# Sharing the gathered value rows between TensorE and VectorE while the second block's coefficients are spread

## The reference, cut to what matters

```
tv, tp = top_k(cand, 16)                    # 8 heads x 16 experts = 128 experts per token
gw = softmax(tv)
a  = einsum('td,ted->te', x, expert_u[ids]) # 128 dot products per token
a  = gelu(a) * gw                           # 128 coefficients per token
out = einsum('te,ted->td', a, expert_v[ids])
```

## Time and profile before

| | |
|---|---|
| median of 3 runs | 2955.72 us (2953.44 to 2956.95) |
| the profiled execution | span 2956.1 us, 0.4 us above the median |
| burst, first to last spreading of block 1 | 2424.8 to 2501.4 us |
| dense product alone on TensorE | 2502.1 to 2936.4 us |
| last instruction of DVE ends | 2953.1 us |

### The profile page before, as it was taken

One profiled execution on the slowest core, in us unless ns is written; L12 is line 12 of the kernel. 1 busy time (PEld: TensorE's weight loads), 2 busy tenths in 40 slices (PEclk: granted clock), 3 DMA queues, 4 the chain that ended last, 5 costly groups with the idle time before them and its releaser, 6 DMA issues.

```text
span 2956.1 us, 31045 instructions
## 1 busy us (share of the span) xinstructions
PE 2663.8 (90%) x11792; PEld 2070.4 (70%) x11792; DVE 2160.4 (73%) x2978; ACT 607.8 (21%) x1271; POOL 894.0 (30%) x712
## 2 busy tenths in 40 slices
PE   6999889999999999999999999667676758999997
PEld 5888678866587588478657688667666755666665
DVE  6787476577896747524677769999999878656667
ACT  1121240110110110122000021122377776000000
POOL 1100001000000100000000024777767657656664
PEclk8999999999999999999999999888877779999998
DMA  9954469868787834324978769999999988999998
GB/s 402 421 190 153 152 226 409 352 247 355 287 319 300 311 128 143 142 100 153 361 279 321 268 273 416 421 421 421 413 421 421 403 338 283 403 410 414 414 414 349
DMA packets 147736, 935.12 MB, mean 316 GB/s; under 512 B 16400, under 2 KB 16656, under 8 KB 53136
## 3 DMA queue, kind: packets, MB, share of 16 engines
q0 software_dynamic: 101376, 604.02, 51.1%
q1 hardware_dynamic: 44784, 320.66, 28.0%
q10 hardware_dynamic: 1440, 8.59, 0.7%
HBM read 929.02 MB, written 4.19 MB: 316 GB/s over the span
## 4 chain that ended last, share of the span: by engine, by line
PE 58%; DMA 19%; DVE 8%; ACT 7%; POOL 5%; issue 3%; DVEq 0%; SPq 0%; ACTq 0%
PE G L579 32%; PE M L894 7%; DMA acc<-v_rows,proj 6%; PE B L894 3%; DMA mix<-v_rows,proj 3%; DMA vec<-peer_u,proj 3%; ACT vec L1576 2%; DMA aring<-peer_u,proj 2%; PE M L1162 2%; DMA proj<-v_rows,proj 2%; DVE vec L2512 2%; PE G L894 2%; POOL aring L551 1%; PE G L1150 1%; POOL acc L563 1%
## 5 line engine op out<-in xcount | busy, mean ns | idle before, releaser
L579 PE MATMUL G<-h,ring 128*128 128x256 f32 x3264 | 715.6, 380 | 0.5 <-ACT h L1298 0.2
L579 PEld LDWEIGHTS G<-h,ring 128*128 128x128 f32 x3264 | 616.1, 190 | 91.6 <-issue 6.8
L536 POOL DMA_DIRECT2D aring<-ada x176 | 93.2, 530 | 1493.7 <-DVE mods L1707 1445.4
L1707 DVE CUSTOM_DVE_ANT_0 aring<-aring,acc,vec 128x2048 f32<-128x2048 f32 x160 | 372.2, 2350 | 49.9 <-DMA aring<-ada 46.8
L579 PE MATMUL G<-proj,ring 128*128 128x256 f32 x1472 | 322.1, 380 | 0.9 <-DVE proj L2324 0.9
L579 PEld LDWEIGHTS G<-proj,ring 128*128 128x128 f32 x1472 | 279.6, 191 | 41.4 <-issue 3.4
L1209 PE MATMUL M<-sq,mix 128*128 128x512 f32 x688 | 301.4, 594 | 0.0
L551 POOL DMA_INDIRECT aring<-peer_u,proj x130 | 228.6, 1759 | 197.2 <-DVE dots L2484 83.3
L1209 PEld LDWEIGHTS M<-sq,mix 128*128 128x128 f32 x688 | 203.6, 297 | 89.3 <-ACT mix L1590 0.7
L2512 DVE SCALAR_TENSOR_TENSOR vec<-acc,dots,vec 128x1024 f32<-128x1024 f32 x149 | 191.5, 1285 | 97.1 <-DMA acc<-v_rows,proj 91.8
L2484 DVE CUSTOM_DVE_ANT_0 aring<-sq,aring 128x2048 f32<-128x2048 f32 x104 | 236.4, 2290 | 29.1 <-DMA aring<-peer_u,proj 18.7
(11 more groups left out here) (494 smaller groups left out, 3670.5 us busy)
## 6 DMA issues: line engine op xcount, KB each, us to landing
ring<-weights SPq DMA_DIRECT2D x219, 1024.0 KB, 5.3
aring<-ada POOLq DMA_DIRECT2D x176, 1024.0 KB, 8.6
sq<-v_blocks SPq DMA_DIRECT2D x43, 1024.0 KB, 8.0
proj<-v_blocks SPq DMA_DIRECT2D x21, 1024.0 KB, 8.0
ring<-first SPq DMA_DIRECT2D x16, 896.0 KB, 11.2
sq<-ada POOLq DMA_DIRECT2D x8, 1024.0 KB, 20.9
acc<-ada POOLq DMA_DIRECT2D x4, 1024.0 KB, 19.4
proj<-ada POOLq DMA_DIRECT2D x4, 1024.0 KB, 22.9
```

The costliest lines, as they stand in the source:

```text
L536: pool.dma_start(ada_at(n), ada[n]).then_inc(ada_in[ada_slot(n)], 16)
L579: mm = nc.tensor.matmul(bank[:, 0:TOK], lhsT=ring[:, slot, weights_at + t * P:weights_at + (t + 1) * P], rhs=rhs[:, t, :], start=(t == ord ...
L1707: V_.tensor_tensor_reduce(out=tile, in0=tile, in1=vector, scale=1.0, scalar=bias, op0=ALU.mult, op1=ALU.add, accum_out=column).then_inc(ad ...
```

## The change

Of block 0's rows, TensorE adds 16 in the burst (the odd rows 1 to 31), one half row in every group. DVE adds the even rows 0 to 30, one in every second group. So the burst adds 32 rows, and the 8 rows from 32 to 39 are added behind it. DVE makes the diagonals instead of ACT, with four buffers instead of two: four of them during the dots (at rows 234 to 240), the others in the burst. DVE marks the one-hot matrices of groups 0 and 1 during the dots (at rows 243 and 247); for that the expert numbers of block 1 are turned ahead of row 239 instead of behind the last row. The diagonal of row 244 is read at row 255 instead of 252. ACT runs a one-column gelu at row 222, right behind the softmax's exponential.

```
+READ_BEHIND[TURN_LATE[-1]] = 255
-V_ON_PE = [4 + 5 * i for i in range(8)]
+V_ON_PE = [1 + 2 * i for i in range(16)]
+IN_BURST = 2 * len(V_ON_PE)
+PICKS_TURNED_AT = TURN_LATE[-2]
+MARKED_AT = {243: 0, 247: 1}
+DIAGS_AT = {234: 0, 236: 1, 238: 2, 240: 3}
+DIAGS = 4
...
 # TensorE: turn_picks(1) ahead of row 239; it waits for mix_in >= 27, no longer for 32
 # turn_coefs(1) waits for mix_in >= 32
+                if n == spreads_after(PICKS_TURNED_AT)[0]:
+                    pe.wait_ge(turned_kept, 3)
+                if n == P // 4 + 1:
+                    pe.wait_ge(turned_kept, 4)
...
             for g in range(P // 4):
                 spread_coefs(1, g)
-                if g % 4 >= 2:
-                    add_row(g // 4, g % 4 - 2)
+                add_row(g // 2, g % 2)
...
 # ScalarE
                 if n == EXP_AT:
                     gate_exp(1)
+                    nc.scalar.activation(small[:, 10:11], eps, ACT.Gelu)
+                if n == PICKS_TURNED_AT - 1:
+                    keep_picks(1)
...
-                if g % 4 == 0:
-                    make_diag(g // 4)
...
 # VectorE
+            def make_diag(i):
+                n = V_ON_PE[i]
+                if i >= DIAGS:
+                    dve.wait_ge(v_summed, i - DIAGS + 1)
+                V_.tensor_scalar(diag(i), ident, dots[:, 1, n // NSLOT, n % NSLOT:n % NSLOT + 1], None,
+                                 ALU.mult).then_inc(diag_made, 1)
...
             for g in range(P // 4):
-                one_hots(g)
-                v_add(in_burst[g])
+                if g >= len(MARKED_AT):
+                    one_hots(g)
+                if g % 2 == 0:
+                    v_add(g)
+                    if g > 0 and g // 2 + DIAGS - 1 < len(V_ON_PE):
+                        make_diag(g // 2 + DIAGS - 1)
...
-            for n in range(P // 4 + len(V_ON_PE), 2 * NSLOT):
+            for n in range(IN_BURST, 2 * NSLOT):
```

More of the change, by code:

```diff
@@ L379, in build @@
         turned_row = acc[:, 1, :]
-        diag = lambda i: proj[:, 37, (i % 2) * P:(i % 2 + 1) * P]
+        diag = lambda i: flat(proj[:, 36:38, :])[:, (i % DIAGS) * P:(i % DIAGS + 1) * P]
         h_late = tiles(sq[:, 0:D], DT)
@@ L1131, in turn_picks @@
                 if tk == 1:
-                    pe.wait_ge(mix_in, P // 4)
+                    pe.wait_ge(mix_in, spreads_after(PICKS_TURNED_AT)[0] - 1)
                 for s in range(2):
@@ L1139, in turn_coefs @@
                 pe.wait_ge(coef_ready, tk + 1)
+                if tk == 1:
+                    pe.wait_ge(mix_in, P // 4)
                 nc.tensor.transpose(G[1][:, 0:P], dots[:, 1, tk, :], ident).then_inc(turned, 1)
@@ L1187, in _ @@
             for n in range(NSLOT + SEL, 2 * NSLOT):
+                if n == PICKS_TURNED_AT:
+                    turn_picks(1)
                 if on_pe(n):
@@ L1191, in _ @@
                         spread_coefs(0, g)
-            turn_picks(1)
             turn_coefs(1)
@@ L1628, in _ @@
                     gate_exp(1)
+                    nc.scalar.activation(small[:, 10:11], eps, ACT.Gelu)
+                if n == PICKS_TURNED_AT - 1:
+                    keep_picks(1)
             keep_mix(0, P // 4 - 1)
-            keep_picks(1)
             dots_gelu(1)
@@ L1642, in weigh_hot @@
                 ins.then_inc(hot_weighed, 1)
[L1644 to L1648, removed]
             act.wait_ge(turned_kept, 4)
@@ L2543, in _ @@
                     coefficients(0)
+                if n in DIAGS_AT:
+                    make_diag(DIAGS_AT[n])
+                if n in MARKED_AT:
+                    dve.wait_ge(turned_kept, 3)
+                    one_hots(MARKED_AT[n])
             coefficients(1)
-            dve.wait_ge(turned_kept, 4)
             dve.wait_ge(mix_in, P // 4)
-            in_burst = [n for n in range(P // 4 + len(V_ON_PE)) if n not in V_ON_PE]
             for g in range(P // 4):
-                one_hots(g)
-                v_add(in_burst[g])
+                if g >= len(MARKED_AT):
[4 more added lines that the diff above has]
+                        make_diag(g // 2 + DIAGS - 1)
             def finish_gathered(tk):
```

## The result

The changed kernel takes 2962.45 us (median of 11 runs, 2959.14 to 2966.61); the kernel before takes 2956.95 us in 11 runs beside them. The ratio is 1.0023, with a 95% interval of 1.0014 to 1.0031: 4 to 9 us slower, 6.8 us by the ratio itself and 5.5 us by the two medians. The forecast was 7.8 us slower.

The account below looks back on a forecast made before the run. TensorE's dense product and the DMA engines' gathers both ran at their limits, with gathered rows ending the kernel. Head -3.3 us plus rows left behind +11.1 gave +7.8 us, 2963.5 us on the median; range 2951 to 2973.

Parts of the forecast that it names:

- The head: Start of the burst, from block 0's last keep_mix to the first scaling (weigh_hot(0)): starts 3.3 us earlier.
- the two transposes: Ahead of row 239, on the TensorE and ScalarE chain ending at 2418.07: they cost 0.5 us.
- The pace: In the burst: VectorE's wait at the diagonal closes a 4.8 us loop over two groups, no faster than today.
- The rows: Behind the burst: 8 more rows left when block loads end, at VectorE's 1.39 us each, 11.1 us.
- The cover: During the dots: added work is hidden, the 1.28 us load in ScalarE's 1.77 us idle time; dots end near 2415.
- rival C: In the burst: late gathers, up to 12 us (2975), or TensorE at the lower clock, 6 us (2970); chance 0.18.

Follow-up runs that it names:

- The head alone: Kernel before plus only expert numbers turned ahead, groups 0 and 1 marked early, one-column gelu, row 244's diagonal read at row 255: 2952.53 us, ratio 0.9989.
- the loosened one: Changed kernel with each diagonal of the burst made two groups later in VectorE's order: 2953.45 us, ratio 0.9996 to the kernel before.
- 24 rows: Changed kernel with 24 rows added in the burst instead of 32, 16 by TensorE and 8 by VectorE: 2976.15 us, ratio 1.0068 to the kernel before.
- The kernel with 40 rows: Changed kernel with 40 rows added in the burst instead of 32, 16 by TensorE and 24 by VectorE: 2988.4 us, ratio 1.0116 to the kernel before.
- the one row added later: Same 40 rows in the burst, but VectorE adds the last of each five one group later: 2958.85 us, ratio 1.0007 to the kernel before.

## Why the prediction was right

The mechanism was right at both of its steps, the loop through the diagonal's buffer and the rows left behind, and each has its own experiment. Step by step, on the forecast's own sum of -3.3 + 11.1 = +7.8:

- *The head.* Forecast: 3.8 us off, less 0.5 for the two transposes. Measured: 4.0 us off (5.42 to 1.40), less 0.37 (the lead of 2.45 us at the fixed row near 2237 is 2.08 at the last copy). The head alone confirms the term: by the profiles the end is 3.7 us earlier with the transposes counted in, where the forecast had 3.3. All kernels with the new head but the loosened one take these 0.36 to 0.38 us more from that row to the last copy. The table load, put at 1.3 us, measured 1.43 us in the kernel without the gelu ahead.
- *The pace.* Forecast: a new loop through the diagonal's wait, 4.8 us for two groups, so that the burst takes as long as before. Measured: 4.84; from the first scaling to the dense product 78.3 us (forecast 78.6, before 78.65). The diagonal lasts 0.28 to 0.29 us but holds VectorE for 0.20. The loosened kernel shows the wait to be the cause. That the 78.6 us came out so closely is in part luck: up to the first waited diagonal it took 7.0 us and not 8.0, since TensorE was back at 1.17 us for the 8 passes in the second group, while the eleven loops took 53.3 instead of 52.8 us and what follows them 18.0 instead of 17.8.
- *The rows.* Forecast: row 36 issued where row 44 was, and 8 rows at VectorE's 1.39 us, 11.1 us. Measured: 36 and 44, and from the start of the dense product to the end 464.5 us instead of 454.0, 10.5. With 24 rows it is 12.4 for the next 8: between the 10.1 and 16 that were the bounds, but above the 11.1, so VectorE's 1.39 us a row is not the whole price there.
- *The cover.* The load at row 222 lies in ScalarE's gap, of which 0.25 us is left. VectorE's dots end at 2410.6, counted as in the kernel before 2413.1, some 2 us earlier than the 2415 I wrote. Why is open: the head alone lacks the wait at row 252 too, and its dots end where those of the kernel before do (176.0 and 175.8 us behind the fixed row, against 173.9 in the changed kernel). Either way they are done before the gelu needs them.

The sum measured is -4.0 + 10.5 = +6.5 us in the profiles (head -4.0, transposes +0.4, the rest of the burst -0.4, rows +10.5) and 0.23% or 6.8 us in the timed runs. The range of 2951 to 2973 was far wider than the miss; it would have held a small gain as well. One test was set wrongly: I had written that a last gather issued less than 5 us later than 2934.5 would show the forecast wrong. It is issued 4.0 us later. The limit was put in absolute time, although executions drift by some us ahead of the burst; by the fixed row it is 6.5 us. Of rival C neither form came about: TensorE's granted clock in the burst rose (0.94 and then 1.00, instead of 0.76 and 0.95), and VectorE waited for no gather until the last groups. The kernel with 40 rows shows what C would have looked like.

## What to carry to other kernels

When work is moved off an engine that sets the pace, follow the new semaphores once round: here VectorE got 0.5 us a group less to do, and one wait for a buffer, placed ahead of the next marking, kept the pace where it was; made a step later, with the same four buffers, it cost nothing. Where one stretch leaves DMA time unused and the next has none, count what is fetched in the first: each gathered row put off cost 1.3 to 1.5 us at the end, about as much as adding it in the burst (1.20 us of VectorE's time). In an order with two consumers and few slots, the row to watch is the one issued behind a slot that the slower engine frees.

## What the runs showed of the hardware that I had not expected

A wait on one engine can cost more than its own length. In the kernel with 40 rows VectorE's waits for gathered rows add up to 27.7 us in the burst, against 7.2 us with the one row added later: 20.5 us more, and yet the burst is 32.7 us longer. Most of the rest is waits for half rows, 14.8 us against 6.8. After 5.14 us of idling TensorE was at its lower level (8 passes in 2.08 us and the half row behind them in 1.91, the 1.2 GHz level, against 1.16 and 1.02 at 2.4 GHz), which is 1.81 us more; and VectorE waited 2.86 us for that half row where it waits 1.05 us in the changed kernel, 1.81 us more.

Executions drift by a few us before the burst begins: in the nine profiles, whose programs are the same up to there, the fixed row near 2237 starts between 2235.7 and 2241.7 us, and block 0's last copy into mix ends between 2412.2 and 2420.9. From that row to the last copy it is 178.9 us in the kernel before and 179.3 us in seven of the other eight, but 176.5 us in the loosened one, although nothing that it changes is run there. What is read from a single profile is safer counted from a point just ahead of the change.
